# Two transformer-style blocks on one core: expert weights read in 16 KB runs, with strided stationary operands in the gather and the transposes

## What is computed

```python
def block(args):
    tids, e, w = args
    xb = x_pad[tids]
    hdn = jax.nn.silu(xb @ w1[e]) * (xb @ w3[e])
    return (hdn @ w2[e]) * w[:, None].astype(xb.dtype)
```

## Time and profile before

| | |
|---|---|
| Time, median of 3 | 1753.53 us (1752.92 to 1755.47) |
| Span of the profiled execution | 1750.7 us |
| TensorE matmul busy | 1594.7 us (91%) |
| TensorE weight load busy (beside the matmuls) | 924.8 us (53%) |
| VectorE, ScalarE, GpSimd busy | 504.9, 407.2, 157.2 us |
| Read from HBM | 500.40 MB |
| Mean granted TensorE clock | 0.957 |
| DMA packets | 208347, of which 207424 on SyncE's queue |

### The profile page before, as it was taken

The page is one execution under the profiler, slowest core; times in us unless marked ns, Lnnn a source line. Parts: engine busy times, 40 slices in busy tenths (PEclk is TensorE's granted clock), DMA queues, the critical chain, the costliest instruction groups (busy, mean ns, idle before and its releaser), DMA issues.

```text
span 1750.7 us, 19525 instructions
## 1 busy us (share of the span) xinstructions
PE 1594.7 (91%) x7964; PEld 924.8 (53%) x7964; DVE 504.9 (29%) x996; ACT 407.2 (23%) x706; POOL 157.2 (9%) x108
## 2 busy tenths in 40 slices
PE   8988999999999996999899999989999496989998
PEld 4554444444434433875544444434434395589986
DVE  0554101010100103034401010100100568567875
ACT  0350111111111112434111111111111252156553
POOL 0110000000000002742000000000000283000000
PEclk9988999999999997989899999999999797999999
DMA  8605999799999999441799979999999640655420
GB/s 326 240 6 211 352 396 393 296 392 397 392 394 395 392 396 340 156 164 43 292 352 395 392 299 397 392 393 397 392 395 383 230 169 24 247 186 178 172 84 24
DMA packets 208347, 502.30 MB, mean 287 GB/s; under 512 B 4000, under 2 KB 5280, under 8 KB 207392
## 3 DMA queue, kind: packets, MB, share of 16 engines
q1 hardware_dynamic: 207424, 495.17, 75.6%
q0 software_dynamic: 864, 6.29, 0.9%
HBM read 500.40 MB, written 1.05 MB: 286 GB/s over the span
## 4 chain that ended last, share of the span: by engine, by line
PE 66%; DMA 18%; DVE 8%; SPq 4%; issue 2%; ACT 2%; PEld 0%; PEldq 0%; DVEq 0%; ACTq 0%
PE bank L805 20%; DMA ring<-in_w_up 17%; PE bank L1054 8%; PE bank L825 6%; PE bank L716 6%; PE bank L683 5%; PE bank L790 4%; SPq L480 4%; PE bank L665 4%; PE bank L1065 3%; PE bank L834 3%; PE bank L781 1%; PE bank L758 1%; PE bank L844 1%; DVE arena L1775 1%
## 5 line engine op out<-in xcount | busy, mean ns | idle before, releaser
L805 PE MATMUL bank<-ring,arena 128*64 128x512 f32 x1792 | 402.8, 605 | 24.2 <-DMA ring<-in_w_up 22.6
L805 PEld LDWEIGHTS bank<-ring,arena 128*64 128x64 f32 x1792 | 135.7, 139 | 286.5 <-issue 286.5
L825 PE MATMUL bank<-ring,arena 128*64 128x512 f32 x896 | 198.4, 594 | 18.3 <-ACT arena L1164 18.3
L1568 DVE TENSOR_TENSOR arena<-arena,bank 128x512 f32<-128x512 f32 x32 | 22.0, 687 | 536.2 <-PE bank L805 536.2
L825 PEld LDWEIGHTS bank<-ring,arena 128*64 128x64 f32 x896 | 74.1, 137 | 124.7 <-issue 124.7
L790 PEld LDWEIGHTS bank<-arena,X 128*128 128x128 f32 x1088 | 124.0, 192 | 26.6 <-issue 26.0
L790 PE MATMUL bank<-arena,X 128*128 128x128 f32 x1088 | 130.5, 278 | 0.3
L834 PE MATMUL bank<-arena 128*128 128x512 f32 x256 | 118.4, 605 | 0.0
L1054 PE MATMUL bank<-x_high,w_high 128*128 128x256 f32 x384 | 109.5, 285 | 4.9 <-DVE x_low L1496 4.9
L1054 PE MATMUL bank<-x_low,w_high 128*128 128x256 f32 x384 | 109.3, 285 | 0.0
L1054 PE MATMUL bank<-x_high,w_low 128*128 128x256 f32 x384 | 109.3, 285 | 0.0
(11 more groups left out here) (297 smaller groups left out, 2083.2 us busy)
## 6 DMA issues: line engine op xcount, KB each, us to landing
ring<-in_w_gate SPq DMA_DIRECT2D x56, 2048.0 KB, 17.4
ring<-in_w_up SPq DMA_DIRECT2D x56, 2048.0 KB, 19.2
ring<-in_w_down SPq DMA_DIRECT2D x56, 2048.0 KB, 17.6
ring<-in_ffn_up SPq DMA_DIRECT2D x12, 2048.0 KB, 9.0
ring<-in_w_in SPq DMA_DIRECT2D x9, 2048.0 KB, 11.5
arena<-in_w_gate SPq DMA_DIRECT2D x6, 2048.0 KB, 16.2
arena<-in_w_up SPq DMA_DIRECT2D x6, 2048.0 KB, 20.4
arena<-in_w_down SPq DMA_DIRECT2D x6, 2048.0 KB, 15.6
```

The lines of the kernel that those rows point to most:

```text
L805: last = nc.tensor.matmul(bank[4 + m][64 * e:64 * e + 64, :], XG[:, c, 64 * e:64 * e + 64], w[e][:, c, :], start=(c == 0), stop=(c == C - 1))
L825: last = nc.tensor.matmul(bank[6 + half][64 * e:64 * e + 64, :], HT[:, j, 64 * e:64 * e + 64], w[e][:, j, 512 * half:512 * half + 512], st ...
```

## The change

`expert_source` now puts rows `p*C + c` (gate, up) and `p*4 + j` (down) at partition `p`. Each partition then reads one run of 16 KB, and a load is 128 runs in place of 1024 (gate, up) or 512 (down). The bytes, the buffers, the waits and the order of the issues are as they were.

Since the features on partition `p` at place `c` are now `p*8 + c`, the gathered tokens have to be laid out alike: `gather` reads as its stationary operand every eighth feature of `X`, 128 elements 32 bytes apart, in place of 128 neighbours. Likewise the transposes of `H` read every fourth element, 16 bytes apart. The counts and shapes of all instructions on all engines are unchanged. `bank`, `XG`, `HT`, and the matmuls at L805, L825, L834 are not touched.

```diff
         def expert_source(l, e, k):
-            if k < 2:
-                return w_gate[l, bass.ds(e, 1)].rearrange("o (c p) f -> p (o c) f", p=P)
-            if k < 4:
-                return w_up[l, bass.ds(e, 1)].rearrange("o (c p) f -> p (o c) f", p=P)
-            return w_down[l, bass.ds(e, 1)].rearrange("o (j p) f -> p (o j) f", p=P)
+            w = (w_gate, w_up, w_down)[k // 2]
+            return w[l, bass.ds(e, 1)].rearrange("o (p c) f -> p (o c f)", p=P)
...
-                sp.dma_start(as_expert(ring[:, slot_no, :], k), expert_source(l, e, k)).then_inc(signal, 16)
+                sp.dma_start(ring[:, slot_no, :], expert_source(l, e, k)).then_inc(signal, 16)
...
                         last = nc.tensor.matmul(bank[6 + c // 4][:, c % 4 * P:(c % 4 + 1) * P],
-                                                X[:, t, c * P:(c + 1) * P], SEL[:, t, :],
+                                                X[:, t, :].rearrange("p (q c) -> p c q", c=C)[:, c, :], SEL[:, t, :],
                                                 start=(t == 0), stop=(t == T - 1))
...
-                    last = nc.tensor.transpose(bank[4][:, j * P:(j + 1) * P], H[:, j * P:(j + 1) * P], ident)
+                    last = nc.tensor.transpose(bank[4][:, j * P:(j + 1) * P], H.rearrange("p (q j) -> p j q", j=FE // P)[:, j, :], ident)
```

More of the change, by code:

```diff
@@ L495, in load_experts @@
                         slot_no = ring_item(l, place) % RING
-                        sp.dma_start(as_expert(ring[:, slot_no, :], k), expert_source(l, e, k))\
+                        sp.dma_start(ring[:, slot_no, :], expert_source(l, e, k))\
                             .then_inc(slot_loaded[slot_no], 16)
                     else:
-                        sp.dma_start(as_expert(FIRST[place - RING], k), expert_source(l, e, k))\
+                        sp.dma_start(FIRST[place - RING], expert_source(l, e, k))\
                             .then_inc(early_loaded[place - RING], 16)
```

## The result

The changed kernel takes 1857.74 us in the median (1857.0 to 1860.7, 4 runs), the kernel before 1754.5 us (1752.92 to 1756.44, 4 runs). The ratio is 1.0593, 95% interval 1.0578 to 1.0608: 5.9% slower, where 1.95% faster was forecast. The time lies 7.7 us above the upper end of the range as well.

What follows compares the result with a forecast made beforehand. DMA bandwidth was taken to bound the late MoE pairs. Layer gains of 16.9 and 17.3 us, sum 34.2, took the 1750.7 us span to 1716.5; adding 2.8 gave 1719.3 us, range 1716 to 1850.

Steps and rivals of the forecast that it cites:

- TensorE's 29.68 us: MoE layers: TensorE's time per pair, to hold for all 16 pairs of a layer once DMA ends no wait.
- The gain of 34.2 us: Both MoE layers: late pairs at TensorE's pace instead of 31.92 us save 16.9 us in layer 1, 17.3 in layer 2.
- The estimate of 426 GB/s: Expert weight loads: DMA rate for 16 KB runs, extended from 387 GB/s at 2 KB and 408 at 4 KB.
- I take zero: Gather on TensorE: strided stationary loads cost nothing more, 3.84 us for 32 records stays; strides-free forecast 51 in 100.
- the first rival: Gather and transposes of H: strided loads run at half speed, covering the DMA gain; 1841 us; 33 in 100.
- the router's 219 ns per record: Router matmuls, where loads set the pace at half clock; used to price half-speed gather loads at 3.2 us more.
- 0.4 us per pair: Transposes of H: most that four strided loads at half speed would add per pair; nothing if strides are free.
- SyncE's queue: Issue of weight loads: two issues hold it 4.37 to 10.01 us; shrinking them was costed at nothing.
- Rivals 2 and 3: Strided loads 10–30 ns/record slower, 1725–1753 us (9 in 100); DMA rate not rising, 1753 or 1731 us (7 in 100).

Runs made afterwards that it cites:

- the kernel with the runs alone: The changed kernel with both stationary operands, X and H, contiguous again, so only the 16 KB runs are left (computation changed): 1719.62 us, ratio 0.9799.
- The stationary sweep: The kernel before, with the gather's eight chunks reading the stationary operand X at strides of 1 to 8 elements, one each: 1814.09 us, one run.
- the moving one: The kernel before, gather's roles swapped: SEL stationary and contiguous, X moving with strides 1 to 8 for its eight chunks: 1810.61 us, one run.
- the gather-only kernel: The kernel before with only the gather's stationary operand taken as every eighth feature, old 2 and 4 KB DMA runs kept: 1857.58 us, ratio 1.0588.

## Why the prediction was wrong

**The bound and the DMA gain were right.** The late pairs were bound by DMA, the rate rose with the length of the runs, and TensorE's 29.68 us is what is left. The gain of 34.2 us and the 1719.3 us are borne out by the kernel with the runs alone, 1719.62 us. The estimate of 426 GB/s lies between the 423 GB/s of its window and the 433 GB/s of the changed kernel's. (By the earlier trace rows it is the first eight pairs and not nine that keep to TensorE's pace; the sum uses the right starts.)

**The step that failed** is the price of the strided stationary operands: "I take zero: a load takes one column in 0.83 ns where the moving side takes one in 0.42, so the memory can deliver twice what a load asks for, and a stride can waste that half unseen." The measured load at stride 8 takes 1.9 ns per column, the gather 4.05 us more. The figure was one of columns, and what counted was pieces of 16 bytes. Neighbours come four to a piece: a load at 0.83 ns per column asks for a piece every 3.3 ns, the moving side at 0.42 for one every 1.7. The stationary sweep puts the least time per piece at 1.7 to 1.9 ns, the moving one at 1.8. So the half was there, and stride 2, which asks for twice the pieces, uses it up: 196 ns in place of 190. Strides 4 and 8 ask for four times as many pieces, and no half covers that. That the moving side's 1.7 ns for neighbours comes from the same limit, and not from its own pace per column, is not shown.

**The rule I set aside was the one that decided.** The sentence on 16-byte lines in the Trainium skill ("SBUF — State Buffer", section Door 1) has it that both reads pay, and it was made the first rival at 33 in 100. Both did: the gather's loads went from 192 to 335 ns, the transposes' from 141 to 208. No row of the trace spoke against it, only the inference above. That there was no room under the matmuls, by the 3.65 of 3.84 us of the earlier trace rows, was right, and was the reason to put more weight there.

**The rival was right in kind and too small.** It said 1841 us. Two of its terms were mis-sized. The gather was priced by the router's 219 ns per record against 120, 3.2 us; it measures 244 against 118, 4.05 us: 34 gathers x 0.85 = 29 us more. The transposes were priced at 0.4 us per pair and cost 0.05: 32 x 0.35 = 11 us less. 1841 + 29 - 11 = 1859, against 1857.74 measured. The router's row shows loads at half the clock; a limit per piece need not be a factor of two, and over the fixed part it was 2.35. The upper end of the range stood on that rival with 9 us to spare, less than the 29 us by which its largest term was off.

**Nothing at SyncE's queue,** as costed: two issues shrank from 4.37 to 10.01 us to 0.8 to 0.9, and the time of the gather-only kernel, with the old issues, is the same as the changed kernel's.

**Rivals 2 and 3** fell: the loads were not slowed slightly but 1.7 times end to end, and the rate rose.

## What to carry to other kernels

A longer DMA run moves the permutation into SBUF, and whoever reads it there pays: in an fp32 matmul keep the innermost step of the operand, stationary or moving, at no more than two elements, or sort the data once with an idle engine. ScalarE did that here in 4 us per layer, where the strided gathers cost 17 times 4.05 us. Where the loads are on the path even two elements are not quite free, 0.20 us per gather here, and a transpose pays some 55 ns per load from stride 2 on.

Before a cost without a row is set to zero, ask whether the rows that seem to exclude it were measured on the same kind of access; a rate in columns, taken from neighbours, is not a rate in separate pieces. And where TensorE's load side is busy 3.65 of 3.84 us, a longer load has nothing to hide under.

## What the runs showed of the hardware that was not expected

- Reads of SBUF by TensorE in fp32 matmuls cost 1.7 to 1.9 ns for each 16-byte piece touched, on both sides alike: records of 128 x 128 follow at 115 to 120 ns up to stride 2, 175 at stride 3, 225 to 240 from stride 4 to 8.
- A transpose's load of 128 columns takes 141 ns for neighbours and 196 to 208 ns for any stride of 2 to 4 elements.
- Loads from HBM run at 387 GB/s in runs of 2 KB, 408 in 4 KB, 413 in a mix of 4 and 8 KB, and up to 433 in 16 KB. A fixed price of about 9 ns per run explains the series within 2%.
